# A triangular inverse on TensorE in tile mode: full-width 128x512 operands against packed 32x32 blocks, with the factor times the inverse carried along

## The reference, cut to what matters

```
decay = jnp.exp(jnp.where(causal, g[..., :, None] - g[..., None, :], -jnp.inf))
lower = jnp.einsum('bhnid,bhnjd->bhnij', k_beta, k) * decay * strict
a_mat = lower + jnp.eye(C, dtype=f32)
rhs = jnp.concatenate([v_beta, k_beta * jnp.exp(g)[..., None]], axis=-1)
sol = lax.linalg.triangular_solve(a_mat, rhs, left_side=True, lower=True, unit_diagonal=True)
...
def step(S, inp):
    v_new = u_c - jnp.einsum('bhck,bhkv->bhcv', w_c, S)
    o = (jnp.einsum('bhck,bhkv->bhcv', q_c * jnp.exp(g_c)[..., None], S)
         + jnp.einsum('bhij,bhjv->bhiv', qk_c, v_new))
    S = S * jnp.exp(gl_c)[..., None, None] + jnp.einsum('bhck,bhcv->bhkv', kt_c, v_new)
```

## Time and profile before

| what | value |
|---|---|
| median of 3 executions | 1916.01 us (1915.22 to 1916.48) |
| profiled execution, its time | 1915.59 us |
| its span | 1913.7 us |
| TensorE matmuls busy | 1868.7 us, 98% |
| VectorE busy | 1554.4 us, 81% |
| ScalarE busy | 859.3 us, 45% |
| GpSimd busy | 775.5 us, 41% |

### The profile page before, as it was taken

The page is one execution under the profiler, slowest core; times in us unless marked ns, Lnnn a source line. Parts: engine busy times, 40 slices in busy tenths (PEclk is TensorE's granted clock), DMA queues, the critical chain, the costliest instruction groups (busy, mean ns, idle before and its releaser), DMA issues.

```text
span 1913.7 us, 35527 instructions
## 1 busy us (share of the span) xinstructions
PE 1868.7 (98%) x13577; PEld 1687.9 (88%) x13577; DVE 1554.4 (81%) x3015; ACT 859.3 (45%) x1507; POOL 775.5 (41%) x579
## 2 busy tenths in 40 slices
PE   6999999999999999999999999999999999999998
PEld 3779999999877899999999888888888888888887
DVE  4577777777766789997895798989989999898998
ACT  3525454444434224488887433433333333343433
POOL 0000000000025434797875254555455655555663
PEclk8999999999999999999999999999999999999999
DMA  9732222222272324766867999999999999999984
GB/s 394 281 107 73 84 73 73 73 84 73 70 286 88 122 78 148 246 195 201 234 204 213 323 377 386 382 390 381 386 375 381 385 394 378 374 372 374 371 338 156
DMA packets 179735, 474.83 MB, mean 248 GB/s; under 512 B 16752, under 2 KB 79184, under 8 KB 176240
## 3 DMA queue, kind: packets, MB, share of 16 engines
q1 hardware_dynamic: 133488, 304.78, 45.3%
q0 software_dynamic: 46080, 167.79, 22.9%
HBM read 426.57 MB, written 45.94 MB: 247 GB/s over the span
## 4 chain that ended last, share of the span: by engine, by line
PE 54%; DVE 10%; DMA 1%; issue 1%; POOL 1%; ACT 0%; DVEq 0%; ACTq 0%
PE dd L2769 17%; PE pp L2756 16%; PE pp L2769 9%; PE pp L2376 7%; PE dd L2724 4%; DMA x<-in_v,idx 1%; POOL hot_a L2536 1%; DVE top_i L2419 1%; DVE top_i L2408 1%; DVE top L3014 1%; DVE less L2409 1%; DVE top_v L2403 1%; DVE top_v L2414 1%; PE pp L465 1%; DVE cand L3126 1%
## 5 line engine op out<-in xcount | busy, mean ns | idle before, releaser
L449 ACT ACTIVATE w_hi<-w_raw 128x1024 fp32r<-128x1024 f32 x202 | 212.8, 1054 | 162.7 <-PE pp L465 106.1
L465 PE MATMUL pp<-act_hi,w_hi 128*128 128x272 f32 x1040 | 236.2, 308 | 2.2 <-ACT qt L2822 1.2
L453 DVE TENSOR_TENSOR w_lo<-w_raw,w_hi 128x1024 fp32r<-128x1024 f32 x173 | 212.3, 1227 | 29.8 <-ACT w_hi L449 29.7
L465 PE MATMUL pp<-act_hi,w_lo 128*128 128x272 f32 x1040 | 214.7, 288 | 0.0
L465 PE MATMUL pp<-act_lo,w_hi 128*128 128x272 f32 x1040 | 214.6, 288 | 0.0
L2951 ACT ACTIVATE co_hi<-cf 128x384 fp32r<-128x384 f32 x126 | 66.3, 527 | 320.9 <-PE pp L2769 257.7
L2756 PE MATMUL pp<-act_hi,w_hi 128*128 128x384 f32 x616 | 208.8, 339 | 0.0
L2756 PE MATMUL pp<-act_lo,w_hi 128*128 128x384 f32 x616 | 207.6, 337 | 0.0
L2756 PE MATMUL pp<-act_hi,w_lo 128*128 128x384 f32 x616 | 207.1, 336 | 0.0
L2536 POOL TENSOR_SCALAR hot_a<-cst,gcols 128x128 f32<-128x128 f32 x144 | 190.2, 1328 | 40.6 <-PE dd L2724 40.2
L3244 DVE TENSOR_TENSOR v_lo<-v_raw,v_hi 128x1024 fp32r<-128x1024 f32 x126 | 153.9, 1221 | 28.3 <-ACT v_hi L2939 26.9
(11 more groups left out here) (485 smaller groups left out, 4615.1 us busy)
## 6 DMA issues: line engine op xcount, KB each, us to landing
w_raw<-in_stream SPq DMA_DIRECT2D x206, 512.0 KB
v_raw<-in_v SPq DMA_DIRECT2D x128, 512.0 KB
ada_w<-in_ada SPq DMA_DIRECT2D x24, 1024.0 KB, 10.4
gt<-gate_matrix SPq DMA_DIRECT2D x31, 768.0 KB
gate_matrix<-gstage SPq DMA_DIRECT2D x11, 2048.0 KB, 10.0
early<-cst SPq DMA_DIRECT2D x50, 192.0 KB
cst<-early SPq DMA_DIRECT2D x50, 192.0 KB
wrow<-in_wout SPq DMA_DIRECT2D x8, 512.0 KB, 8.2
```

The costliest lines, as they stand in the source:

```text
L449: nc.scalar.activation(w_hi[k.slot][:], w_raw[k.slot][:], ACT.Copy).then_inc(w_hi_done, 1)
L453: nc.vector.tensor_tensor(w_lo[k.slot][:], w_raw[k.slot][:], w_hi[k.slot][:].bitcast(F32), ALU.subtract).then_inc(w_lo_done, 1)
L465: last = nc.tensor.matmul(pp[s][:, b, 0:HN], w[:, c * P:(c + 1) * P], a[:, c, b * HN:(b + 1) * HN], start=(c == 0 and w is w_hi[s] and a i ...
```

## The change

The blocks of 32 that the first levels work on are packed: the diagonal 32x32 blocks of the 4 chunks stand side by side, so that an operand of levels 0 to 3 is 128x128 (TC = 128 columns) and not 128x512. With the transposed inverse `ty[:, 0]`, its product with the factor, `ty[:, 1]`, is carried: one product on TensorE (`products`) makes it at the start, and in each of levels 0 to 2 one call of `correct(2)` corrects both by matmuls of twice the columns; level 3 corrects the inverse alone (`correct(1)`). VectorE subtracts the correction, transposes the carried product (`yl`) and masks it (`apc`). The 32-blocks are joined to 64 by tiles off the diagonal (`a4`, then three small products for each chunk), and 64 to 128 as before, from `ti_lo`. The two copies `a4` and `a5` are ScalarE's. Seven constants are folded to 32 columns at the start of the block, on VectorE (`folded_c`). The transposes of v (line 1311) move behind level 3. PIECES is dealt out anew, with the same sum. GpSimd clears one tile of 128x256 in place of six of 128x512.

```diff
-        PIECES = {"start": 4, "beta": 1, "turned": 2, "inverse": 2,
-                  **{f"level {n}": 3 for n in range(NLV - 1)}, **{f"after {n}": 1 for n in range(NLV - 1)},
-                  f"level {NLV - 1}": 2, f"after {NLV - 1}": 1, "scan 0": 1, "state 0": 1,
+        PIECES = {"start": 4, "beta": 1, "turned": 2, "inverse": 2, "products": 3, "level 0": 4, "level 1": 3, "level 2": 3,
+                  "level 3": 3, "level 4": 1, "joined 4": 3, "level 5": 2, "joined 5": 1, "scan 0": 1, "state 0": 1,
...
+        def correct(columns):
+            for c in range(NC):
+                t = strip(c)
+                for b in range(4):
+                    r = strip(b)
+                    if columns == 2:
+                        out, right = by_two(dd[r, 2, 0:2 * TC])[:, :, t], ty[r, :, t]
+                    else:
+                        out, right = dd[r, 2, t], ty[r, 0, t]
+                    last = nc.tensor.matmul(out, apc[r, t], right, start=True, stop=True, tile_position=(B4 * b, B4 * b))
...
# TensorE
+                    for c in range(NC):
+                        for b in range(4):
+                            r, t = strip(b), strip(c)
+                            last = nc.tensor.matmul(dd[r, 1, t], tic[r, t], ltc[r, t], start=True, stop=True,
+                                                    tile_position=(B4 * b, B4 * b))
+                    last.then_inc(y_done, 1)
+                    beside("products")
+                    for n in range(N32):
+                        gate_pe(pe, ty_ready, (N32 + 2) * hv + n + 2)
+                        pe.wait_ge(ap_ready, N32 * hv + n + 1)
+                        correct(2 if n < N32 - 1 else 1).then_inc(dty_done, 1)
+                        beside(f"level {n}")
...
+                    for c in range(NC):
+                        for b in (1, 3):
+                            t = c * P + B4 * b
+                            last = nc.tensor.matmul(dd[strip(b), 1, strip(c)], lt[strip(b - 1), t:t + B4],
+                                                    tic[strip(b - 1), strip(c)], start=True, stop=True,
+                                                    tile_position=(B4 * (b - 1), B4 * b))
+                    beside("level 4")
...
+                    for c in range(NC):
+                        t = strip(c)
+                        nc.tensor.matmul(dd[strip(1), 2, t], ty[strip(1), 0, t], a4[strip(1), t], start=True, stop=True,
+                                         tile_position=(B4, B4))
+                        for b in (3, 1):
+                            last = nc.tensor.matmul(dd[strip(b - 1), 3, t], a4[strip(b), t], ty[strip(b), 0, t], start=True,
+                                                    stop=True, tile_position=(B4 * b, B4 * (b - 1)))
+                    beside("joined 4")
+                    (level 5: four 64x64 products a5 from lt and ti_lo, two pieces, four from a5 and tu, one piece)
...
# VectorE
+                    for b in range(4):
+                        last = nc.vector.tensor_tensor(by_chunk(ltc[strip(b), :]), in_chunks(dd[strip(b), 2, :], b),
+                                                       in_chunks(decay[strip(b), :], b), ALU.mult)
...
+                    for n in range(N32):
+                        if n == 0:
+                            nc.vector.tensor_copy(ty[:, 1], dd[:, 1, 0:TC]).then_inc(ty_ready, 1)
+                        else:
+                            nc.vector.tensor_tensor(ty[:], ty[:], by_two(dd[:, 2, 0:2 * TC]), ALU.subtract).then_inc(ty_ready, 1)
+                        nc.vector.transpose(yl[:], ty[:, 1]).then_inc(yl_ready, 1)
+                        nc.vector.tensor_tensor(by_chunk(apc[:]), by_chunk(yl[:]), to_chunks(folded_c[:, LOW_C + n]),
+                                                ALU.mult).then_inc(ap_ready, 1)
+                        if n < 3:
+                            inside(n)
+                        beside(("inverse", "level 0", "level 1", "level 2")[n])
```

More of the change, by code:

```diff
@@ L1052, in b_tile, with strip, by_chunk, in_chunks @@
             return a.unsqueeze(1).to_broadcast([P, NC, P])
-        B2 = P // 2
-        B4 = P // 4
-        def diagonal_blocks(bank, left, right, size=B2):
-            for c in range(NC):
[L1062 to L1065, removed]
-            return last
[L1068 to L1085, removed]
+        B2, B4 = P // 2, P // 4
+        TC = NC * B4
+        N32 = 4
+        LO, HI = slice(0, B2), slice(B2, P)
+        def strip(b):
+            return slice(B4 * b, B4 * (b + 1))
+        def by_chunk(t):
+            return t.rearrange("p (c n) -> p c n", c=NC)
+        def in_chunks(t, b):
+            return by_chunk(t)[:, :, strip(b)]
+        def to_chunks(a):
+            return a.unsqueeze(1).to_broadcast([P, NC, B4])
+        EYE_C, PAIR_C, LOW_C, OWN_C = 0, 1, 2, 2 + N32
+        def correct(columns):
+            for c in range(NC):
+                t = strip(c)
[6 more added lines that the diff above has]
+                    last = nc.tensor.matmul(out, apc[r, t], right, start=True, stop=True, tile_position=(B4 * b, B4 * b))
+            return last
+        def by_two(t):
+            return t.rearrange("p (h n) -> p h n", h=2)
         def heads_in_turn(eng, first, turn, finish):
@@ L1153, in _ @@
                 retire(pool, ended)
-                for n in range(NLV):
-                    nc.gpsimd.memset(ap_[n][:], 0.0).then_inc(ap_zero, 1)
+                nc.gpsimd.memset(ti_lo[:], 0.0).then_inc(ti_zero, 1)
                 def keep(k, col):
@@ new lines, in head @@
+                    last.then_inc(t21_done, 1)
+                    beside("joined 4")
+                    pe.wait_ge(ti_ready, 3 * hv + 3)
+                    for c in range(NC):
+                        t = slice(c * B2, (c + 1) * B2)
+                        last = nc.tensor.matmul(dd[HI, 1, t], lt[LO, c * P + B2:(c + 1) * P], ti_lo[LO, t],
+                                                start=True, stop=True)
+                    last.then_inc(a5_done, 1)
+                    beside("level 5")
@@ new lines, in head @@
+                    pe.wait_ge(tu_ready, 2 * hv + 1)
+                    gate_pe(pe, a5_ready, hv + 1)
+                    for c in range(NC):
+                        t = slice(c * B2, (c + 1) * B2)
+                        last = nc.tensor.matmul(dd[LO, 3, t], a5[HI, t], tu[HI, c * P + B2:(c + 1) * P],
+                                                start=True, stop=True)
+                    last.then_inc(t5_done, 1)
+                    beside("joined 5")
+                    pe.wait_ge(tu_ready, 2 * hv + 2)
@@ new lines, in head @@
+                    if not has_prior(hv):
+                        dve.wait_ge(ti_zero, 1)
+                    dve.wait_ge(ti_ready, 3 * hv + 2)
+                    for b in range(2):
+                        nc.vector.tensor_copy(by_chunk(ti_lo[strip(b), :])[:, :, strip(b)], by_chunk(tic[strip(b), :]))
+                    inside(3)
+                    beside("level 3")
+                    dve.wait_ge(t21_done, hv + 1)
+                    nc.vector.tensor_scalar(by_chunk(ti_lo[strip(1), :])[:, :, strip(0)], by_chunk(dd[strip(1), 2, 0:TC]), -1.0, None,
+                                            ALU.mult).then_inc(ti_ready, 1)
```

138 lines of the change are left out of this document (70 added, 68 removed).

## The result

The changed kernel takes 1896.1 us (median of 4 executions, 1894.93 to 1897.16), the kernel before 1915.62 us (4 executions) beside it. The ratio is 0.990, with a 95% interval from 0.988 to 0.992: 19.5 us faster. The forecast was 1897.0, with a range from 1890 to 1907. The profiled execution took 1896.67 us with a span of 1894.9, so the spans differ by 18.8 us.

A forecast was written before the change was run, and what follows sets the result against it. TensorE's queue was taken to bound the kernel (busy 98% of the span). Shorter visits 15.7 plus waits 4.4 less start of the block 1.5 gave 18.6 us saved from 1915.6, so 1897.0 us, range 1890 to 1907.

The forecast's parts named there:

- TensorE's queue is the time: Block of the heads: as long as TensorE's queue, so a microsecond taken out saves one if no other queue becomes late.
- Removed, 8.60 us a head: TensorE, per head: 12 old tile-mode visits go, seven 32x32 at 0.58 us each, the rest at levels 0, 4 and 5.
- Added, 6.64 us a head: TensorE, per head: nine new tile-mode visits, from the first product through corrections and joins to level 5.
- The wide correction at 0.82: Each `correct(2)` visit, levels 0 to 2: 0.82 us, since its busiest tile streams what it does in a 64x64 visit.
- the joins: Level 4's three joins: two tiles on the same rows stream one after the other, 0.82 us; 0.58 if together.
- VectorE keeps up: Levels 0 to 3: every wait has 0.8 us in hand; VectorE's inverse work falls from 10.9 to about 9.2 us a head.
- The nine waits, 4.4 us: TensorE's nine waits ahead of the tile products, 4.4 us in all eight heads, taken as gone.
- The start of the block, 1.5 us: Seven new VectorE reductions ahead of normalised q and k: 7 x 0.2 + 0.1 = 1.5 us lost, bounds 0.7 and 2.1.
- Wide corrections nearly free: Rival: visits bound by issue, a doubled visit costs 0.63 us, joins 0.58; 25.1 us saved, 1890.5 us. Chance 0.20.
- Slack eaten: Rival: packed 32-column operands cost VectorE 0.35 us more a level; 4 to 10 us back, 1901 to 1907. Chance 0.17.
- slower: Rival: VectorE becomes the bound from level 0 to 3, lists 1.2 us longer a level; 10 us slower, 1926 us. Chance 0.05.
- Turns at the bank: No-change rival: row tiles take turns at their bank where columns are doubled; 14.6 us back, 1911.6 us. Chance 0.06.

The follow-up runs named there:

- the split corrections: Changed kernel with each of the three wide corrections of a head done in two visits, two chunks each: 1905.33 us, ratio 0.995.
- the sets of 32 columns: Changed kernel with the three joins of 32-blocks issued six times (1910.96 us), or two of them five times extra, on the same rows (1904.99) or different rows and columns (1905.94).
- the second series: Runs measured beside the kernel before at 1915.58 us: changed kernel again (1895.85 us), joins six times (1910.96), extra VectorE work once a head (1895.83) or at every level (1899.59).

## Why the prediction was right

**TensorE's queue is the time.** Right. The gain in the six middle heads is 2.79 us each (heads are 50.52 us apart, and 51.3 was forecast). Of that the visits give 8.60 - 6.23 = 2.37 and the wait that is gone 0.34; the last 0.08 is not placed. More products in a visit and more visits each cost their own price, and 0.57 us more of VectorE once a head cost nothing.

**Removed, 8.60 us a head.** This was read off the trace of before, and nothing contradicts it.

**Added, 6.64 us a head: measured 6.23.** 0.58 + 3 x 0.78 + 0.58 + 0.55 + 0.58 + 0.79 + 0.80 = 6.22; level 4's product is 0.55 after the transposes of v are taken out. The wide correction at 0.82 was near (0.78). The term of this sum that was mis-sized is the joins: "one after the other they stream 16 instructions of 32 columns", 0.82; it was 0.58, since tiles on the same rows don't take turns (0.25 us a set with shared and with own rows). So 2.4 us a head was saved and not 1.96, 19 us in eight heads and not 15.7.

**The price of a visit.** The runs give it two parts: about 0.33 us for going into tile mode and back (0.32 by the split corrections, 0.58 - 0.25 by the sets of 32 columns), and eight instructions in the busiest tile at 31 ns each with 32 columns (0.25) or 55 with 64 (0.44). The old kernel: 12 x 0.33 + 7 x 0.25 + 6 x 0.44 = 8.4, the new one: 9 x 0.33 + 4 x 0.25 + 5 x 0.44 = 6.2. The sums of the prediction's single readings are 8.60 and 6.23, so the two parts are good to some 0.25 us a head. Of the 2.2 that they give, 1.0 is fewer visits and 1.2 is less in them: fewer visits alone are not half of the saving. The Trainium skill (TensorEngine Tiling (Array Packing), Key Properties) says that changing the mode drains TensorE. These runs fit that, with 0.32 us for each further visit of the same products, but none of them shows what TensorE does in that time. As a price, the rule of the Trainium skill's same page on row tiles and PSUM banks doesn't hold in them: a wide correction, 32 instructions of 64 columns from four row tiles into one bank, costs 0.78 us, as level 5's visit with eight such instructions in a single tile does (0.79).

**VectorE keeps up.** Right, with more room than forecast: slack 1.2 us at the least and not 0.8. A dependent instruction starts 0.03 us after the one before it has ended and not 0.11. On the other side the four strips took 1.19 us and not 0.9: they followed each other at 0.30 and did not overlap. All in all VectorE's busy time fell less than forecast, from 40.3 to 39.3 us a head (mean of two heads in the middle), 1.0 less, where the step from "10.9 us" to "9.2" made 1.7.

**The nine waits, 4.4 us.** Mostly right. None stands ahead of a tile product now, but in the last head, where it was 0.69 us (a mask on VectorE stood behind two taps and a low half), the wait became one of the projection for that low half, 0.73 us.

**The start of the block, 1.5 us.** This was the worst term: 2.24 us more of wait (2.69 less 0.45), outside its own bounds of 0.7 to 2.1, and behind it matmuls at the 1.2 GHz level. With both it took about 3.1 us, as the second head's start shows (0.8 us gained where 2.4 from the visits and 1.7 from waits were due, less 0.2 by which the block began later). The step that failed is "7 x 0.2", borrowed from another operation: the reductions took 1.68 us for six, 0.28 each, the wait behind them 0.33 and not 0.1, and the clock had no term.

**The sum.** 18.6 forecast, 18.8 by the spans. That it is so near is partly luck: 3.3 us more from the visits stand against 1.6 at the start of the block, 0.7 of a wait that moved, 0.4 of a longer wait behind the heads and 0.4 in the rest. In the second series the start of the block cost 1.3 us more.

**The rivals.** Wide corrections nearly free: fell (0.78, not 0.63), though one of its two terms, the joins at 0.58, came true. Slack eaten, and slower: neither came, as every mask was 1.2 us early or more; they were not far off either, since four more instructions a head on VectorE brought a wait of 0.5 us. Turns at the bank: fell (0.44 us for a second set of 32 wide instructions).

## What to carry to other kernels

Where TensorE's queue is the time and tiles alternate with full-width work, price a visit as an entry (0.33 us here) plus the busiest tile's stream. From that it follows that products should be spread over tiles until the busiest has as few as possible; shared rows or banks cost nothing here, shared columns were not tried. Before placing set-up work ahead of the first operands of a block, see who waits for them: a new wait of 2 us can also cost the clock behind it, though not in every execution. A walk through the queues with the durations of the old trace told the slack of the new kernel to 0.4 us; the same walk for four more instructions a head forecast 9 us where 3.7 came.

## What the runs showed of the hardware that was not expected

- Three tiles with 24 instructions, two tiles on the same rows with 16, and two on their own rows with 16 all cost 0.25 us a set: the busiest tile's eight instructions set it.
- Behind a wait of 2.7 us without a matmul the granted clock fell to the 1.2 GHz level for some microseconds in seven of ten profiles and stayed at 1.00 in three; behind 0.46 us it stayed at 1.00. It cost 1.1, 2.4 and 0 us in the three that were worked out. A wait of 2.02 us later in the program was followed by the lower level in one profile, one of 2.31 us in the same place in another was not.
- Four tensor_tensor instructions on 32 partitions that read `dd` took 1.19 us, 0.30 each, and six tensor_reduce of 128x128 took 1.68, 0.28 each; the tensor_scalar of 128x128 in the earlier trace rows came to 0.22, and so did two copies on 32 partitions (0.43 for both). So it is not the 32 partitions; what it is was not tried.
- With 144 instructions of joins in one visit three heads had a halt of 1.38, 0.84 and 0.64 us, whose cause stays open.
